# Splitting all 24 weight pieces of a mixture-of-experts step, with the second activation half converted one piece earlier

## The chip, the cores and the metric

The kernel runs on one core of a Trainium2 chip. The metric is the time on the device in microseconds (us) of one execution of the whole block; the shown time of a kernel is the median of its runs. The profile is one further execution, taken by the hardware profiler, which has a time of its own.

## The reference

One decoder layer with 1024 tokens and a width of 1024, all in float32. First a mixer (attention with a window of 128, and a linear recurrent branch, joined by gates), then a mixture of experts, then a last RMSNorm. The change touches the mixture of experts alone:

```python
logits = t @ w_router + b_router
top_val, top_idx = lax.top_k(logits, 4)          # 4 of 32 experts for each token
gate = softmax(top_val)
# for each expert e and its tokens xc, in chunks of 128 rows
gu = xc @ w_gate_up[e] + b_gate_up[e]            # 1024 -> 2048
g, u = gu[:, :1024], gu[:, 1024:]
g = minimum(g, 7); u = clip(u, -7, 7)
act = (u + 1) * (g * sigmoid(1.702 * g))
y = act @ w_down[e] + b_down[e]                  # 1024 -> 1024
out[token] += gate * y
```

## The kernel before, in words

**Steps.** After the mixer and the router the kernel runs a loop of steps (the loops `Fori(0, MAXS // 2)`, two steps u = 0, 1 in each turn, the guard `If(j < total)`). A step is one expert with up to 128 of its tokens. With these inputs there are 32 steps, one for each expert. An expert that has between 1 and 32 tokens more than a chunk holds has these computed in the same step as its tail (`If(tail > 0)`), by products of 32 rows each (`tail_product`, L676). Five engines run the same list of steps, each with its own program, and meet at semaphores.

**Weights.** An expert has six units of weights of 2 MB: units 0 and 2 are the gate columns, 1 and 3 the up columns, 4 and 5 the down projection. SyncE requests them by DMA (L362) into `ring`, each as soon as the step before has done with the same unit (`unit_mm[i]`). A unit is used in four pieces of 128x1024 numbers, which are numbered n = 0 to 23 in the order of their use (`sub_unit`): pieces 0 to 3 are unit 0, 4 to 7 unit 1, 8 to 11 unit 2, 12 to 15 unit 3, and 16 to 23 alternate in pairs between units 4 and 5.

**Split pieces.** A piece is multiplied by the rows of the tokens in one of two ways. A *split* piece is written as a high part and the remainder, both of type float32r: ScalarE copies the piece from `ring` to `w_hi` (function `high`, L900), VectorE subtracts that copy from the piece and writes `w_lo` (`low`, L1463), and TensorE runs six matmuls of 512 columns: twice rows_hi by w_hi, rows_lo by w_hi (L659, L660), and rows_hi by w_lo (L663). The buffers `w_hi` and `w_lo` have four places (NBUF = 4), so `high` of a piece waits (`sub_mm`) until TensorE has finished the split piece four before it. The rows themselves were split in the same way at the start of the step (`rows_hi` L892, `rows_lo` L1467), and so is the activation, in two halves: `actT_out` writes `act_hi` (ScalarE, L923), `actT_low` writes `act_lo` (VectorE, L1509).

**Native pieces.** Pieces 7 and 15 (`NATIVE`) are not split. TensorE multiplies them straight from `ring` as float32 (L650), by `rows_f`, a plain float32 copy of the last 256 contraction rows that ScalarE makes for each step (L891, in `rowsT_out`). Nothing is converted for these two; `SPLIT` lists the 22 others, and the index m of a piece in that list numbers the buffers and the semaphore counts.

**What else the engines do between pieces.** Everything is written out by hand, in program order on each engine; n is the piece after whose conversion, or before whose product, the work stands.

- TensorE, before piece n: n = 12 and n = 18: waits for half 0 or 1 of the activation (`act_done`) and transposes it (L687). n = 16 and n = 20: waits for `act_lo_done` of half 0 or 1. n = 16 also: two tail products. n = 20 also: transposes the rows of the next step (L621). After the last piece of a unit: a bias product (L642), which raises `unit_mm`.
- ScalarE, after `high` of piece n: n = 8: sigmoid of gate half 0 (L919). n = 16: `actT_out(0)`, then the sigmoid of gate half 1. n = 21: `actT_out(1)`. After piece 23: the rows of the next step, its pieces 0 to 3, and the two halves of the output (L927).
- VectorE, after `low` of piece n: n = 9: gate part 0 (L1483, L1485). n = 11: up part 0 (L1490, L1492). n = 16: `actT_low(0)`. n = 17: gate part 1. n = 18: up part 1, whose last instruction (L1492) raises `act_done` for the transposes before piece 18. n = 19: the tail's part. n = 21: `actT_low(1)`. After piece 23: `rows_lo` of the next step and its pieces 0 to 3.

```python
# TensorE, L683 on                              # ScalarE, L899
if n in ACT_T:        # (12, 18)                act.wait_ge(sub_mm, j * NSP + m + 1)
    pe.wait_ge(act_done, j * 2 + half + 1)      # VectorE, L1462
    ... 4 transposes, L687                      dve.wait_ge(hi_done, j * NSP + m + 1)
```

Of the kernel before, what the change touches and what calls it, by code (L numbers as in the profile page):

```python
# [6 lines left out]
P = 128  # L7
NT = SEQ // P
KD = D // P
HALF = 512  # L10
# [15 lines left out]
SUBS = 24  # L26
NATIVE = (7, 15)
SPLIT = tuple(n for n in range(SUBS) if n not in NATIVE)
NSP = len(SPLIT)
NBUF = 4  # L30
# [14 lines left out]
def hybrid_decoder_block(nc, x, positions, norm_mix_g, w_in, conv_w, conv_b, w_rg, b_rg, w_ig, b_ig,  # L45
# [25 lines left out]
    with ctx:  # L71
# [130 lines left out]
        rows_f = take(2 * P)  # L202
# [201 lines left out]
        def _(pe):  # L404
            mm = nc.tensor.matmul
# [229 lines left out]
            with pe.Fori(0, MAXS // 2) as pair:  # L635
                for u in range(2):
                    j = pair * 2 + u
                    with pe.If(j < total):
# [6 lines left out]
                        def piece(n):  # L645

                            i, k0 = sub_unit(n)
                            if n in NATIVE:
                                for q in range(2):
                                    last = mm(bank(i), rows_f[:, q * P:(q + 1) * P], wu[i][:, k0 + q, :], start=False, stop=False)  # L650
                            else:
                                m = SPLIT.index(n)
                                buf = (m + u * NSP) % NBUF
                                hi, lo = (rows_hi, rows_lo) if i < 4 else (act_hi, act_lo)
                                pe.wait_ge(hi_done, j * NSP + m + 1)
                                for q in range(2):
                                    ks = slice((k0 + q) * P, (k0 + q + 1) * P)
                                    wh = w_hi[:, buf, q * HALF:(q + 1) * HALF]
                                    mm(bank(i), hi[:, ks], wh, start=(k0 + q == 0), stop=False)  # L659
                                    mm(bank(i), lo[:, ks], wh, start=False, stop=False)  # L660
                                pe.wait_ge(lo_done, j * NSP + m + 1)
                                for q in range(2):
                                    last = mm(bank(i), hi[:, (k0 + q) * P:(k0 + q + 1) * P], w_lo[:, buf, q * HALF:(q + 1) * HALF],  # L663
                                              start=False, stop=False)
                                last.then_inc(sub_mm, 1)
                            if k0 + 2 == KD:
                                if i == 0:
                                    pe.wait_ge(sel_ready, j + 1)
                                bias(bank(i), i, 0, HALF, P).then_inc(unit_mm[i], 1)
# [56 lines left out]
        def _(act):  # L726
# [163 lines left out]
            def rowsT_out():  # L890
                act.activation(rows_f, bank(7)[:, 2 * P:4 * P], ACT.Copy)  # L891
                act.activation(rows_hi[:], bank(6, 2), ACT.Copy).then_inc(rowsT_done, 1)  # L892

            def high(m, u, j):

                i, k0 = sub_unit(SPLIT[m])
                if k0 == 0:
                    wait_reg(act, w_arrived[i], j * 16 + 16)
                act.wait_ge(sub_mm, j * NSP + m + 1)  # L899
                act.activation(w_hi[:, (m + u * NSP) % NBUF, :], place[i][:, k0 * HALF:(k0 + 2) * HALF], ACT.Copy).then_inc(hi_done, 1)  # L900

# [3 lines left out]
            for m in range(NBUF):  # L905
                high(m, 0, 0)
# [4 lines left out]
            with act.Fori(0, MAXS // 2) as pair:  # L911
                for u in range(2):
                    j = pair * 2 + u
                    with act.If(j < total):
# [14 lines left out]

                        for m in range(NBUF, NSP):  # L930
                            n = SPLIT[m]
                            high(m, u, j)
# [13 lines left out]
                            if n == 21:  # L946
                                actT_out(1)
# [3 lines left out]
                        with act.If(more > 0):  # L951
                            wait_reg(act, rowsT_mm, j + 2)
                            rowsT_out()
                            high(0, 1 - u, j + 1)
                        wait_reg(act, added, j * 16 + 16)
                        output(0)
                        with act.If(more > 0):
                            high(1, 1 - u, j + 1)
                            high(2, 1 - u, j + 1)
                        output(1)  # L960
                        with act.If(more > 0):
                            high(3, 1 - u, j + 1)
# [182 lines left out]
        def _(dve):  # L1145
# [312 lines left out]
            def low(m, u, j):  # L1458

                i, k0 = sub_unit(SPLIT[m])  # L1460
                buf = (m + u * NSP) % NBUF
                dve.wait_ge(hi_done, j * NSP + m + 1)  # L1462
                v.tensor_tensor(out=w_lo[:, buf, :], in0=place[i][:, k0 * HALF:(k0 + 2) * HALF],  # L1463
                                in1=w_hi[:, buf, :].bitcast(f32), op=ALU.subtract).then_inc(lo_done, 1)
# [8 lines left out]
            for m in range(NBUF):  # L1473
                low(m, 0, 0)
            with dve.Fori(0, MAXS // 2) as pair:
                for u in range(2):
                    j = pair * 2 + u
                    with dve.If(j < total):
# [34 lines left out]
                        for m in range(NBUF, NSP):  # L1513
                            n = SPLIT[m]
                            low(m, u, j)
# [15 lines left out]
                            if n == 21:  # L1531
                                actT_low(1)
                        with dve.If(more > 0):
                            dve.wait_ge(rowsT_done, j + 2)
                            rows_low()
                            for m in range(NBUF):
                                low(m, 1 - u, j + 1)
# [38 lines left out]
```

## Time and profile before

| | |
|---|---|
| median of 3 runs | 2251.74 us (2250.1 to 2253.74) |
| the profiled execution: its own time | 2247.22 us |
| the profiled execution: span of the core | 2245.6 us |
| mean granted clock of TensorE | 0.971 of 2.4 GHz |
| busy over the span: TensorE, VectorE, ScalarE, GpSimd | 94%, 66%, 53%, 13% |
| the 32 steps of experts | from 810 us to 2208 us of the span |

How to read it: the span runs from the first instruction of the program to the last. "PE" is TensorE's matmuls, "PEld" its loads of stationary operands, "DVE" VectorE, "ACT" ScalarE, "POOL" GpSimd, "SP" SyncE. An engine's busy time is what its records cover. Records of following instructions of one engine overlap a little, so the pace of an engine is read from start to start. L1463 is line 1463 of the kernel before.

### The profile page before, as it was taken

The page shows a single profiled execution, that of the slowest core. Times are in us where ns is not written, and L with a number is a line of the kernel's source. Part 1 is how long each engine was busy: PE and PEld are TensorE (multiplying, and loading weights), DVE is VectorE, ACT ScalarE, POOL GpSimd, SP SyncE. Part 2 cuts the span into 40 slices and gives each one's busy share as a digit, 9 for nine tenths or more (in the row PEclk, how much of TensorE's full clock was granted, in tenths as well). Part 3 has the DMA queues.
Part 4 walks back from the last instruction along what each step waited for, and adds up shares of the span by engine and source line. Part 5 has one row for each costly group of instructions (what it writes and reads, how often), then busy time and mean ns, then how long its engine had stood idle before and what let it go on. Part 6 is the DMA issues. An engine that isn't in the chain of part 4 may idle for free.

```text
span 2245.6 us, 35483 instructions
## 1 busy us (share of the span) xinstructions
PE 2109.2 (94%) x11224; PEld 1474.1 (66%) x11225; DVE 1491.8 (66%) x1900; ACT 1195.0 (53%) x1623; POOL 282.7 (13%) x334
## 2 busy tenths in 40 slices
PE   7989988999989669999999999999999999999993
PEld 4445555767668547777777677776777777776772
DVE  4326654555444557877877668977877887876784
ACT  3152434334333336666756557766665766765674
POOL 3010000000002410110222101111211010210000
PEclk9999999999999779999999999999999999999997
DMA  7110020110043576987977779978979979976994
GB/s 224 38 38 0 22 75 1 38 38 19 20 169 113 157 228 227 353 297 277 371 271 255 245 280 380 373 261 285 355 252 332 370 264 375 345 256 242 373 344 158
DMA packets 247678, 489.51 MB, mean 218 GB/s; under 512 B 19915, under 2 KB 29991, under 8 KB 247536
## 3 DMA queue, kind: packets, MB, share of 16 engines
q1 hardware_dynamic: 218768, 439.37, 54.2%
q0 software_dynamic: 21088, 49.35, 8.3%
q10 hardware_dynamic: 7776, 0.19, 0.2%
q8 instruction: 27, 0.44, 0.1%
q14 instruction: 19, 0.16, 0.0%
HBM read 461.01 MB, written 32.05 MB: 220 GB/s over the span
## 4 chain that ended last, share of the span: by engine, by line
PE 90%; DVE 4%; issue 3%; DMA 1%; SPq 1%; ACT 1%; POOL 0%; POOLq 0%; ACTq 0%; DVEq 0%
PE psum L659 15%; PE psum L660 14%; PE psum L663 14%; PE psum L676 8%; PE psum L427 5%; PE psum L552 5%; PE psum L650 5%; PE psum L540 3%; PE psum L542 3%; PE psum L535 3%; PE psum L642 2%; PE psum L451 2%; PE psum L495 2%; PE psum L621 2%; PE psum L597 1%
## 5 line engine op out<-in xcount | busy, mean ns | idle before, releaser
L1463 DVE TENSOR_TENSOR w_lo<-ring,w_hi 128x1024 fp32r<-128x1024 f32 x704 | 850.3, 1222 | 162.8 <-ACT w_hi L900 142.1
L900 ACT ACTIVATE w_hi<-ring 128x1024 fp32r<-128x1024 f32 x704 | 741.0, 1061 | 349.2 <-PE psum L663 337.4
L659 PE MATMUL psum<-w_hi,rows_hi 128*128 128x512 f32 x896 | 372.1, 415 | 4.2 <-DVE rows_lo L1467 2.7
L660 PE MATMUL psum<-w_hi,rows_lo 128*128 128x512 f32 x896 | 350.4, 391 | 0.0
L663 PE MATMUL psum<-w_lo,rows_hi 128*128 128x512 f32 x896 | 277.0, 390 | 0.0
L659 PE MATMUL psum<-w_hi,act_hi 128*128 128x512 f32 x512 | 220.0, 430 | 0.3 <-issue 0.3
L659 PEld LDWEIGHTS psum<-w_hi,rows_hi 128*128 128x128 f32 x896 | 169.5, 189 | 52.2 <-issue 20.9
L660 PE MATMUL psum<-w_hi,act_lo 128*128 128x512 f32 x512 | 202.4, 395 | 0.0
L663 PEld LDWEIGHTS psum<-w_lo,rows_hi 128*128 128x128 f32 x896 | 168.5, 188 | 36.2
L660 PEld LDWEIGHTS psum<-w_hi,rows_lo 128*128 128x128 f32 x896 | 169.2, 189 | 32.9
L676 PE MATMUL psum<-ring,region_m 128*32 128x256 f32 x3072 | 174.2, 380 | 0.0
L663 PE MATMUL psum<-w_lo,act_hi 128*128 128x512 f32 x512 | 160.9, 395 | 0.0
L1295 DVE TENSOR_TENSOR h_lo<-ring,h_hi 128x1024 fp32r<-128x1024 f32 x64 | 78.4, 1225 | 118.3 <-ACT g_hi L822 118.3
L1131 POOL DMA_INDIRECT acc_rows<-region_m,meta x32 | 53.6, 1676 | 804.3 <-ACT region_m L927 734.7
L676 PEld LDWEIGHTS psum<-ring,region_m 128*32 128x32 f32 x3072 | 95.9, 110 | 73.5 <-issue 13.8
L819 ACT ACTIVATE h_hi<-ring 128x1024 fp32r<-128x1024 f32 x64 | 68.1, 1064 | 136.6 <-PE psum L542 136.6
L650 PE MATMUL psum<-ring,region_a 128*128 128x512 f32 x256 | 120.2, 592 | 0.0
L659 PEld LDWEIGHTS psum<-w_hi,act_hi 128*128 128x128 f32 x512 | 96.9, 189 | 27.9 <-issue 10.4
L663 PEld LDWEIGHTS psum<-w_lo,act_hi 128*128 128x128 f32 x512 | 96.2, 188 | 23.3
L552 PE MATMUL psum<-ring 128*128 128x512 f32 x256 | 111.2, 592 | 0.0
L427 PE MATMUL psum<-ring 128*128 128x512 f32 x256 | 110.1, 592 | 0.8 <-DVE ring L1167 0.8
L660 PEld LDWEIGHTS psum<-w_hi,act_lo 128*128 128x128 f32 x512 | 96.7, 189 | 17.8
(289 smaller groups left out, 2747.8 us busy)
## 6 DMA issues: line engine op xcount, KB each, us to landing
ring<-in_w_gate_up_dram SPq DMA_DIRECT2D x128, 2048.0 KB, 14.9
ring<-in_w_down_dram SPq DMA_DIRECT2D x64, 2048.0 KB, 11.4
ring<-in_w_in_dram SPq DMA_DIRECT2D x9, 1024.0 KB, 8.1
ring<-in_w_in_dram SPq DMA_DIRECT2D x3, 2048.0 KB, 22.8
region_m<-in_x_dram SPq DMA_DIRECT2D x8, 512.0 KB, 9.8
ring<-in_w_out_dram SPq DMA_DIRECT2D x2, 2048.0 KB, 7.6
region_a<-in_x_dram POOLq DMA_DIRECT2D x8, 512.0 KB, 4.7
acc_rows<-region_a POOLq DMA_DIRECT2D x8, 512.0 KB, 2.9
```

Of the source, the lines that this page charges most:

```text
L427: last = mm(bank(4 + n % 4), w[:, k, m * P:(m + 1) * P], hT[:, k, th * HALF:(th + 1) * HALF], start=(k == 0), stop=(k == KD - 1))
L535: mm(bank(2 * th + q), g_hi[b][:, q * P:(q + 1) * P], h_hi[b][:, th * HALF:(th + 1) * HALF], start=first, stop=False)
L552: last = mm(bank(4 + 2 * th + q), w[:, k, j * P:(j + 1) * P], x_[:, k, th * HALF:(th + 1) * HALF], start=(k == 0), stop=(k == GROUP - 1))
L650: last = mm(bank(i), rows_f[:, q * P:(q + 1) * P], wu[i][:, k0 + q, :], start=False, stop=False)
L659: mm(bank(i), hi[:, ks], wh, start=(k0 + q == 0), stop=False)
L660: mm(bank(i), lo[:, ks], wh, start=False, stop=False)
L663: last = mm(bank(i), hi[:, (k0 + q) * P:(k0 + q + 1) * P], w_lo[:, buf, q * HALF:(q + 1) * HALF], start=False, stop=False)
L676: mm(dst[TAIL * q:TAIL * (q + 1), :], stat_of(k), wu[i][:, k, c:c + QC], start=(k == 0), stop=False)
L819: act.activation(h_hi[b][:], hT[:, k, :], ACT.Copy)
L900: act.activation(w_hi[:, (m + u * NSP) % NBUF, :], place[i][:, k0 * HALF:(k0 + 2) * HALF], ACT.Copy).then_inc(hi_done, 1)
L1295: v.tensor_tensor(out=h_lo[b][:], in0=hT[:, k, :], in1=h_hi[b][:].bitcast(f32), op=ALU.subtract)
L1463: v.tensor_tensor(out=w_lo[:, buf, :], in0=place[i][:, k0 * HALF:(k0 + 2) * HALF], in1=w_hi[:, buf, :].bitcast(f32), op=ALU.subtract).then ...
```

## The change

All 24 pieces of a step become split pieces. `NATIVE`, `SPLIT`, `NSP`, the copy `rows_f` and its conversion are gone; the buffer of a piece is n % 4, and the semaphore counts go by 24 in a step. `actT_out(1)` on ScalarE and `actT_low(1)` on VectorE stand after piece 20, where they stood after piece 21. The order of TensorE's work stays, except that pieces 7 and 15 are six float32r matmuls each.

```diff
--- before.py
+++ after.py
@@ -24,9 +24,6 @@
 UNIT = KD * HALF
 SHIFT = 4
 SUBS = 24
-NATIVE = (7, 15)
-SPLIT = tuple(n for n in range(SUBS) if n not in NATIVE)
-NSP = len(SPLIT)
 NBUF = 4
 TAIL_ROWS_AT, TAIL_GU_AT, TAIL_ACT_AT, NEXT_ROWS_AT = 13, 16, 21, 20
 ACT_T = (12, 18)
@@ -199,7 +196,6 @@
         gsig = [take(HALF) for _ in range(2)]
         act_rows = [take(HALF) for _ in range(2)]
         glu = take(HALF)
-        rows_f = take(2 * P)
         tail_sig, tail_act, tail_glu, yrow_t = (take(QC) for _ in range(4))
         assert at[0] <= A_COLS - 2 * D
 
@@ -645,24 +641,19 @@
                         def piece(n):
 
                             i, k0 = sub_unit(n)
-                            if n in NATIVE:
-                                for q in range(2):
-                                    last = mm(bank(i), rows_f[:, q * P:(q + 1) * P], wu[i][:, k0 + q, :], start=False, stop=False)
-                            else:
-                                m = SPLIT.index(n)
-                                buf = (m + u * NSP) % NBUF
-                                hi, lo = (rows_hi, rows_lo) if i < 4 else (act_hi, act_lo)
-                                pe.wait_ge(hi_done, j * NSP + m + 1)
-                                for q in range(2):
-                                    ks = slice((k0 + q) * P, (k0 + q + 1) * P)
-                                    wh = w_hi[:, buf, q * HALF:(q + 1) * HALF]
-                                    mm(bank(i), hi[:, ks], wh, start=(k0 + q == 0), stop=False)
-                                    mm(bank(i), lo[:, ks], wh, start=False, stop=False)
-                                pe.wait_ge(lo_done, j * NSP + m + 1)
-                                for q in range(2):
-                                    last = mm(bank(i), hi[:, (k0 + q) * P:(k0 + q + 1) * P], w_lo[:, buf, q * HALF:(q + 1) * HALF],
-                                              start=False, stop=False)
-                                last.then_inc(sub_mm, 1)
+                            buf = n % NBUF
+                            hi, lo = (rows_hi, rows_lo) if i < 4 else (act_hi, act_lo)
+                            pe.wait_ge(hi_done, j * SUBS + n + 1)
+                            for q in range(2):
+                                ks = slice((k0 + q) * P, (k0 + q + 1) * P)
+                                wh = w_hi[:, buf, q * HALF:(q + 1) * HALF]
+                                mm(bank(i), hi[:, ks], wh, start=(k0 + q == 0), stop=False)
+                                mm(bank(i), lo[:, ks], wh, start=False, stop=False)
+                            pe.wait_ge(lo_done, j * SUBS + n + 1)
+                            for q in range(2):
+                                last = mm(bank(i), hi[:, (k0 + q) * P:(k0 + q + 1) * P], w_lo[:, buf, q * HALF:(q + 1) * HALF],
+                                          start=False, stop=False)
+                            last.then_inc(sub_mm, 1)
                             if k0 + 2 == KD:
                                 if i == 0:
                                     pe.wait_ge(sel_ready, j + 1)
@@ -888,22 +879,21 @@
 
 
             def rowsT_out():
-                act.activation(rows_f, bank(7)[:, 2 * P:4 * P], ACT.Copy)
                 act.activation(rows_hi[:], bank(6, 2), ACT.Copy).then_inc(rowsT_done, 1)
 
-            def high(m, u, j):
-
-                i, k0 = sub_unit(SPLIT[m])
+            def high(n, j):
+
+                i, k0 = sub_unit(n)
                 if k0 == 0:
                     wait_reg(act, w_arrived[i], j * 16 + 16)
-                act.wait_ge(sub_mm, j * NSP + m + 1)
-                act.activation(w_hi[:, (m + u * NSP) % NBUF, :], place[i][:, k0 * HALF:(k0 + 2) * HALF], ACT.Copy).then_inc(hi_done, 1)
+                act.wait_ge(sub_mm, j * SUBS + n + 1)
+                act.activation(w_hi[:, n % NBUF, :], place[i][:, k0 * HALF:(k0 + 2) * HALF], ACT.Copy).then_inc(hi_done, 1)
 
             act.sem_inc(y_done)
             act.sem_inc(ty_done)
             act.activation(ssq[:, 2, 0:1], eps, ACT.Sigmoid)
-            for m in range(NBUF):
-                high(m, 0, 0)
+            for n in range(NBUF):
+                high(n, 0)
             act.wait_ge(rowsT_mm, 1)
             rowsT_out()
             act.wait_ge(table_done, 1)
@@ -927,9 +917,8 @@
                             act.activation(yrow[u][:, half * HALF:(half + 1) * HALF], bank(4 + half), ACT.Copy,
                                            scale=meta[:, u, 1:2].bitcast(f32)).then_inc(y_done, 1)
 
-                        for m in range(NBUF, NSP):
-                            n = SPLIT[m]
-                            high(m, u, j)
+                        for n in range(NBUF, SUBS):
+                            high(n, j)
                             if n == 8:
                                 sigmoid(0)
                             if n == 16:
@@ -943,7 +932,7 @@
                                 with act.If(tail > 0):
                                     wait_reg(act, tgate_mm, before + 2)
                                     act.activation(tail_sig, bank(1)[:, 0:QC], ACT.Sigmoid, scale=ALPHA).then_inc(tgsig_done, 1)
-                            if n == 21:
+                            if n == 20:
                                 actT_out(1)
                         with act.If(tail > 0):
                             wait_reg(act, tactT_mm, before + 1)
@@ -951,15 +940,15 @@
                         with act.If(more > 0):
                             wait_reg(act, rowsT_mm, j + 2)
                             rowsT_out()
-                            high(0, 1 - u, j + 1)
+                            high(0, j + 1)
                         wait_reg(act, added, j * 16 + 16)
                         output(0)
                         with act.If(more > 0):
-                            high(1, 1 - u, j + 1)
-                            high(2, 1 - u, j + 1)
+                            high(1, j + 1)
+                            high(2, j + 1)
                         output(1)
                         with act.If(more > 0):
-                            high(3, 1 - u, j + 1)
+                            high(3, j + 1)
                         with act.If(tail > 0):
                             wait_reg(act, tdown_mm, before + 2)
                             wait_reg(act, tadded, before * 16 + 16)
@@ -1455,13 +1444,12 @@
             def selector(u, e):
                 v.tensor_copy(sel_cur[0:96, u, :], eq[0:96, ds(e, 1)].to_broadcast([96, P])).then_inc(sel_ready, 1)
 
-            def low(m, u, j):
-
-                i, k0 = sub_unit(SPLIT[m])
-                buf = (m + u * NSP) % NBUF
-                dve.wait_ge(hi_done, j * NSP + m + 1)
-                v.tensor_tensor(out=w_lo[:, buf, :], in0=place[i][:, k0 * HALF:(k0 + 2) * HALF],
-                                in1=w_hi[:, buf, :].bitcast(f32), op=ALU.subtract).then_inc(lo_done, 1)
+            def low(n, j):
+
+                i, k0 = sub_unit(n)
+                dve.wait_ge(hi_done, j * SUBS + n + 1)
+                v.tensor_tensor(out=w_lo[:, n % NBUF, :], in0=place[i][:, k0 * HALF:(k0 + 2) * HALF],
+                                in1=w_hi[:, n % NBUF, :].bitcast(f32), op=ALU.subtract).then_inc(lo_done, 1)
 
             def rows_low():
                 v.tensor_tensor(out=rows_lo[:], in0=bank(6, 2), in1=rows_hi[:].bitcast(f32),
@@ -1470,8 +1458,8 @@
             selector(0, 0)
             dve.wait_ge(rowsT_done, 1)
             rows_low()
-            for m in range(NBUF):
-                low(m, 0, 0)
+            for n in range(NBUF):
+                low(n, 0)
             with dve.Fori(0, MAXS // 2) as pair:
                 for u in range(2):
                     j = pair * 2 + u
@@ -1510,9 +1498,8 @@
                                             in1=act_hi[:, half * HALF:(half + 1) * HALF].bitcast(f32),
                                             op=ALU.subtract).then_inc(act_lo_done, 1)
 
-                        for m in range(NBUF, NSP):
-                            n = SPLIT[m]
-                            low(m, u, j)
+                        for n in range(NBUF, SUBS):
+                            low(n, j)
                             if n == 4:
                                 selector(1 - u, e_next)
                             if n == 9:
@@ -1528,13 +1515,13 @@
                             if n == 19:
                                 with dve.If(tail > 0):
                                     tail_glu_part()
-                            if n == 21:
+                            if n == 20:
                                 actT_low(1)
                         with dve.If(more > 0):
                             dve.wait_ge(rowsT_done, j + 2)
                             rows_low()
-                            for m in range(NBUF):
-                                low(m, 1 - u, j + 1)
+                            for n in range(NBUF):
+                                low(n, j + 1)
                         dve.nop()
 
             for t in range(NT):
```

## Rows read from the trace of the kernel before

**Rows 1.** The page: busy time of TensorE, and the shares of the last chain.

```profile
PE 2109.2 (94%) x11224; PEld 1474.1 (66%) x11225; DVE 1491.8 (66%) x1900; ACT 1195.0 (53%) x1623; POOL 282.7 (13%) x334
...
PE 90%; DVE 4%; issue 3%; DMA 1%; SPq 1%; ACT 1%; POOL 0%; POOLq 0%; ACTq 0%; DVEq 0%
```

**Rows 2.** Windows: PE, PEld, DVE, ACT, POOL busy us (records), PE clock, DMA share, GB/s.

```profile
1435.85:1473.21 37.36, 37.07 (x164) 28.13 (x164) 33.37 (x35) 27.65 (x30) 6.84 (x9) 1.00 1.04 370
1473.21:1523.31 50.10, 49.68 (x378) 35.12 (x378) 37.68 (x41) 29.84 (x35) 8.80 (x10) 1.00 0.72 251
```

**Rows 3.** Groups by line: busy us, mean ns of one, then idle before them.

```profile
L1463 DVE TENSOR_TENSOR w_lo<-ring,w_hi 128x1024 fp32r<-128x1024 f32 x704 | 850.3, 1222 | 162.8 <-ACT w_hi L900 142.1
...
L676 PE MATMUL psum<-ring,region_m 128*32 128x256 f32 x3072 | 174.2, 380 | 0.0
...
L650 PE MATMUL psum<-ring,region_a 128*128 128x512 f32 x256 | 120.2, 592 | 0.0
```

**Rows 4.** Timeline of TensorE, step without tail: start us, us, operation, idle before.

```profile
1453.46 0.60 PE L687 MATMUL psum<-ident,region_a 128*128 128x128 f32 x4
...
1455.29 0.39 PE L659 MATMUL psum<-w_hi,rows_hi 128*128 128x512 f32 x1
...
1456.65 0.39 PE L659 MATMUL psum<-w_hi,rows_hi 128*128 128x512 f32 x1
...
1458.01 1.88 PE L650 MATMUL psum<-ring,region_a 128*128 128x512 f32 x4
1459.73 0.38 PE L642 MATMUL psum<-region_s,region_m 96*128 96x512 bf16 x1
...
1461.34 0.40 PE L659 MATMUL psum<-w_hi,act_hi 128*128 128x512 f32 x1
...
1462.74 0.60 PE L687 MATMUL psum<-ident,region_a 128*128 128x128 f32 x4
...
1466.43 1.06 PE L621 MATMUL psum<-ident,region_m 128*128 128x128 f32 x8 [0.29 <-issue]
```

**Rows 5.** Timeline of ScalarE in the same step.

```profile
1453.43 1.06 ACT L900 ACTIVATE w_hi<-ring 128x1024 fp32r<-128x1024 f32 x1 [0.30 <-PE psum L663]
1454.40 0.58 ACT L923 ACTIVATE act_hi<-psum 128x512 fp32r<-128x512 f32 x1
1454.87 0.59 ACT L919 ACTIVATE region_a<-psum 128x512 f32<-128x512 f32 x1
1455.49 1.06 ACT L900 ACTIVATE w_hi<-ring 128x1024 fp32r<-128x1024 f32 x1
```

**Rows 6.** Timeline of VectorE in the same step.

```profile
1449.60 0.69 DVE L1492 SCALAR_TENSOR_TENSOR region_a<-region_a 128x512 f32<-128x512 f32 x1
...
1456.59 1.22 DVE L1463 TENSOR_TENSOR w_lo<-ring,w_hi 128x1024 fp32r<-128x1024 f32 x1 [0.24 <-ACT w_hi L900]
1457.73 0.42 DVE L1483 TENSOR_SCALAR region_a<-region_a 128x512 f32<-128x512 f32 x1
1458.18 0.69 DVE L1485 SCALAR_TENSOR_TENSOR region_a<-psum,region_a 128x512 f32<-128x512 f32 x1
1458.79 1.22 DVE L1463 TENSOR_TENSOR w_lo<-ring,w_hi 128x1024 fp32r<-128x1024 f32 x1
1460.15 0.69 DVE L1490 TENSOR_SCALAR region_a<-psum 128x512 f32<-128x512 f32 x1
1460.87 0.69 DVE L1492 SCALAR_TENSOR_TENSOR region_a<-region_a 128x512 f32<-128x512 f32 x1
```

**Rows 7.** Timeline at the first step's start, granted clock at its lower level.

```profile
808.72 1.23 DVE L1467 TENSOR_TENSOR rows_lo<-psum,rows_hi 128x1024 fp32r<-128x1024 f32 x1 [22.36 <-ACT rows_hi L892]
...
810.08 0.79 PE L659 MATMUL psum<-w_hi,rows_hi 128*128 128x512 f32 x1 [2.73 <-DVE rows_lo L1467]
...
811.09 0.63 PE L659 MATMUL psum<-w_hi,rows_hi 128*128 128x512 f32 x1
...
811.52 0.63 PE L660 MATMUL psum<-w_hi,rows_lo 128*128 128x512 f32 x1
```

## The prediction

> **What bounds the kernel now.** I read the page first: TensorE is busy for 94% of the span, and the chain that ended last is 90% TensorE [rows 1]. Over a stretch such a share can hide much, so I then looked at single steps. There are two kinds. A native piece leaves four records on L650, so its 256 records are 64 pieces, two in each of 32 steps; a tail leaves 192 records on L676, so its 3072 are 16 tails [rows 3]. Sixteen steps have a tail and take about 50 us, sixteen have none and take 37.4 us [rows 2]. In both TensorE is covered but for 0.3 to 0.4 us. So in the expert loop the product stream sets the time, and a microsecond taken out of it counts, as long as nothing else is late.
>
> How near is the next engine? In the step without tail VectorE is busy 33.37 of 37.36 us, in the one with tail 37.68 of 50.10 [rows 2]. The reader should see that the two kinds differ: in one VectorE has 4 us to spare, in the other 12. For a sum over a whole step 4 us are plenty; for a chain of dependent work inside it they need not be, and the change touches such a chain.
>
> **Part 1: the products.** A split piece takes TensorE 1.36 us from start to start (1455.29 to 1456.65), a native one 1.72 us (1458.01 to 1459.73) [rows 4]. Each of the 64 exchanged pieces saves 0.36 us: 0.72 us in each step, 23.0 us in all, if TensorE never waits.
>
> The Trainium skill ("TensorE: Matmul & The Clock Gate", Back-to-back issue gap) gives about 216 ns for an isolated 512-column matmul at full clock, against the 227 ns that 1.36 / 6 makes here. By it a split piece would be 1.29 us and the saving 27 us; the row decides.
>
> **Part 2: the conversions.** Each step gains two `high` (1.06 us) on ScalarE and two `low` on VectorE. The record of a `low` is 1.22 us, but back to back its pace is 1.14 us (1456.59 to 1457.73) [rows 6]. VectorE's load without tail rises from 33.4 to 35.7 us against a TensorE step of 37.36 - 0.72 = 36.64 us. As a sum it still fits, and with a tail easily. ScalarE, 27.65 us busy [rows 2], has room for 2.1 us more. The removed copy `rows_f` hid behind products; I cost it at nothing.
>
> **Part 3: the chain to the transposes before piece 18.** These wait for `act_done`, raised by the last L1492. Today that ends at 1461.56 and the transposes start at 1462.74 [rows 6, 4]: slack 1.18 us. Two things lengthen the chain. `high(16)` waited for the fourth *split* piece back, which was piece 11, because 15 was skipped; now it is piece 12. And `high(17)` stands behind `high(16)`, `actT_out(0)` and the sigmoid. Today these three ran early, and `high(17)` could start 0.20 us after piece 12 ended (1455.49 against 1455.29) [rows 5, 4]. Let P be the end of piece 12. After the change:
>
> - ScalarE: `high(16)` at P + 0.20, `actT_out(0)` 0.97 later, the sigmoid 0.47 later, `high(17)` 0.49 later (a record of 0.59 less the 0.10 by which its neighbours overlap), so at P + 2.13; it ends at P + 3.19 [rows 5].
> - VectorE: `low(17)` at P + 3.23, then 1.14 to L1483, 0.45 to L1485, 0.61 to `low(18)`, 1.14 to L1490, 0.72 to L1492 and 0.69 for itself [rows 6]: P + 7.98.
> - TensorE asks for it at P + 7.45 today (1462.74 - 1455.29), and at P + 7.09 with piece 15 shorter [rows 4].
>
> Add 0.13 us from VectorE's end to TensorE's start (809.95 to 810.08) [rows 7], and TensorE waits 7.98 + 0.13 - 7.09 = 1.02 us. No row of before shows that wait, so I bound it. With no delay at the semaphore it is 0.89 us. With every record laid end to end without overlap (0.20 + 1.06 + 0.58 + 0.59 + 1.06 + 0.04 + 1.22 + 0.42 + 0.69 + 1.22 + 0.69 + 0.69 = 8.46) it is 1.50 us. I take 1.02, since starts in the rows show the overlap at each of these pairs. Queued behind this wait are pieces 18 to 23 and the whole next step, so it counts in full. It comes once in each step without tail. In a step with tail two tail products stand between pieces 15 and 16, 174.2 / 48 = 3.6 us each [rows 3]; in these 7.2 us the chain finishes, and the step keeps its 0.72 us.
>
> The transposes before piece 12 wait in the same way for the first half, whose L1492 ends at 1450.29 and which is wanted at 1453.46 [rows 6, 4]: 3.17 us of slack. The added `low(7)` moves it back by 1.14 us and TensorE comes 0.36 us earlier; some 1.6 us are left, and I cost it at nothing.
>
> **Part 4: the moved half.** Piece 20 waits for `act_lo_done` of half 1. With the wait above, the transposes start at P + 8.11, and TensorE stands before piece 20 about 3.2 us later, P + 11.3 (today L621, just behind that point and with 0.29 us of idle time ahead of it, starts 3.69 us after the transposes) [rows 4]. ScalarE's `actT_out(1)` waits for the transposes and ends near P + 9.3; VectorE goes `low(19)` P + 7.9, `low(20)` 9.0, `actT_low(1)` 10.2 to 10.9. It is in time by 0.4 us. Behind `low(21)`, at its old place, it would be at 12.0 and cost another 0.7 us. So the move saves a new wait rather than time of before: nothing in the sum. On ScalarE `high(21)` stands behind that wait, and is 1 us later than it could be; piece 21 comes only near P + 14, so nobody feels it. No DMA is moved; SyncE's requests follow `unit_mm` and come earlier or later with TensorE.
>
> **The sum.** 32 x 0.72 = 23.0 us gained, 16 x 1.02 = 16.3 us given back: 6.7 us less. The profiled execution would go from 2247.2 to 2240.5 us. It lies 4.5 us under the median of the runs shown, so the median goes from 2251.7 to 2245.0 us. Steps without tail become 0.3 us *longer* (37.7), steps with tail 0.7 us shorter (49.4). About 0.2%, or 4.5 us, is what a measurement can tell from no change, and the forecast is just beyond it.
>
> **The rivals.**
>
> *The whole saving arrives.* If the chain were 1 us shorter than I add it up, TensorE would not wait: -23.0 us, 2229. For it: VectorE's sum fits, and TensorE waits for neither engine inside a step today. Against it: the rows give every link. A ceiling may also step in: without tail DMA already moves 370 GB/s at a share of 1.04 [rows 2], so a step of 36.64 us needs 2% more than it delivers now. Anything from 2229 to 2241: 0.18.
>
> *The wait is longer and eats the gain.* With 1.3 to 1.7 us in each of 16 steps the sum is -2.2 to +4.2 us. The end-to-end bound is 1.50. 0.12.
>
> *A second wait, and the kernel is slower.* The margin before piece 20 is 0.4 us. If `actT_low(1)` came 1.14 us later than worked out, one `low`, TensorE would wait 0.7 us more in each step without tail: -6.7 + 16 x 0.74 = +5.1 us, 2257. It decides from 0.4 us of lateness on, and the kernel is slower by over 0.2% from 0.7 us of added waiting. For it: VectorE at 35.7 of 37 us has hardly a pause in which to catch up. Against it: in the rows it does catch up before piece 20. 0.08.
>
> *The clock falls.* Today the granted clock is 1.00 in these stretches and TensorE's gaps are 0.3 us [rows 2, 4]. If idle microseconds in every step sent it to its lower level, a matmul would take 0.43 us (811.09 to 811.52) [rows 7] instead of 0.23: six pieces at it, 36 x 0.20, are 7 us in a step without tail, 16 x 7 - 7 = +105 us in all, 2357. One wait of 1 us in 37 is little beside what TensorE does around it, so 0.02. The Trainium skill ("TensorE: Matmul & The Clock Gate", A second HAM failure mode) describes such an oscillation with frequent short idles between groups of matmuls; no row here shows one in the loop.
>
> **How the numbers follow.** My own case, one wait of 0.8 to 1.3 us before piece 18, has 0.60 and spans -10.2 to -2.2 us: 2241.5 to 2249.5. The range 2233 to 2254 takes in the longer wait and half of the larger gains; outside stay the full gain (0.10) and the two slow cases (0.10). Faster by over 0.2% needs a wait under 18.5 / 16 = 1.16 us: 0.44 of my 0.60, and the first rival's 0.18, make 0.62. Same: 0.16 + 0.12 = 0.28. Slower: 0.10.
>
> **What would show it.** In the profile after, L650 and L891 are gone, and L900 and L1463 count 768. The group L687 shows idle time before it, released by VectorE's L1492 of before, 16 times about 1 us and never in a step with tail. Steps without tail take 37.7 us, with tail 49.4. No idle time released by `act_lo`, none by DMA. I am wrong if L687 shows no wait (full gain), if L621 or piece 20 shows one (second rival on the slow side), or if the steps with tail gain less than 0.7 us.

## The result, and the profile after

The changed kernel takes 2230.7 us (median of 6 runs, 2229.8 to 2231.3) against 2251.7 us for the kernel before on the same chip. The ratio is 0.9905, with a 95% interval of 0.9892 to 0.9918: 21 us less, between 18 and 24. The forecast was 2245.0 us, range 2233 to 2254. The direction was right; the gain is three times the one worked out, and outside the range.

The profiled execution took 2230.5 us. From its page, the lines that answer to [rows 1] and to the first of [rows 3]:

```profile
PE 2088.0 (94%) x11352; PEld 1494.9 (67%) x11353; DVE 1550.9 (70%) x1964; ACT 1244.1 (56%) x1655; POOL 291.4 (13%) x334
...
PE 84%; DVE 5%; issue 4%; ACT 2%; DMA 2%; SPq 1%; POOL 0%; ACTq 0%; DVEq 0%; POOLq 0%
...
L1451 DVE TENSOR_TENSOR w_lo<-ring,w_hi 128x1024 fp32r<-128x1024 f32 x768 | 915.0, 1221 | 144.2 <-ACT w_hi L890 132.7
```

TensorE's busy time fell by 21.2 us, and its share of the last chain from 90% to 84%: something else now stands in that chain. Next, two steps of the same kinds as in [rows 2], with the same columns:

```profile
1428.43:1465.72 37.29, 36.56 (x168) 28.62 (x168) 34.96 (x37) 29.00 (x31) 8.18 (x9) 1.00 1.05 374
1465.72:1514.72 49.00, 48.80 (x383) 35.89 (x382) 39.60 (x43) 31.46 (x36) 9.26 (x10) 1.00 0.74 255
```

The step without tail went from 37.36 to 37.29 us (forecast 37.7), the one with tail from 50.10 to 49.00 us (forecast 49.4). Both are 0.4 us shorter than forecast. With 16 steps of each kind that makes 16 x 0.07 + 16 x 1.10 = 18.7 us. (These are single steps; the 16 steps with tail take 799.8 us in the trace of before and 781.6 us in this one, 1.14 us less each.)

**The wait that was forecast is there.** First the changed kernel's group of transposes (L678 answers to L687), then timelines of the three engines in the step without tail, as in [rows 4 to 6]:

```profile
its engine sat idle before it (us, times) until:
  DVE region_a L1480: 30.4, 32
```

The 32 times are 16 waits, each counted once for the matmuls (16 times 0.73 us, 11.7 us) and once for the loads of the stationary operands.

```profile
1447.52 0.39 PE L650 MATMUL psum<-w_hi,rows_hi 128*128 128x512 f32 x1
...
1453.24 0.39 PE L650 MATMUL psum<-w_hi,act_hi 128*128 128x512 f32 x1
...
1455.54 0.66 PE L678 MATMUL psum<-ident,region_a 128*128 128x128 f32 x4 [0.73 <-DVE region_a L1480]
1455.95 0.48 PE L650 MATMUL psum<-w_hi,act_hi 128*128 128x512 f32 x1
...
1458.93 1.06 PE L617 MATMUL psum<-ident,region_m 128*128 128x128 f32 x8
```

```profile
1447.72 1.06 ACT L890 ACTIVATE w_hi<-ring 128x1024 fp32r<-128x1024 f32 x1 [1.00 <-PE psum L654]
1448.69 0.58 ACT L913 ACTIVATE act_hi<-psum 128x512 fp32r<-128x512 f32 x1
1449.17 0.59 ACT L909 ACTIVATE region_a<-psum 128x512 f32<-128x512 f32 x1
1449.64 2.01 ACT L890 ACTIVATE w_hi<-ring 128x1024 fp32r<-128x1024 f32 x2
```

```profile
1450.73 1.23 DVE L1451 TENSOR_TENSOR w_lo<-ring,w_hi 128x1024 fp32r<-128x1024 f32 x1
...
1454.79 0.69 DVE L1480 SCALAR_TENSOR_TENSOR region_a<-region_a 128x512 f32<-128x512 f32 x1
...
1457.67 0.68 DVE L1497 TENSOR_TENSOR act_lo<-psum,act_hi 128x512 fp32r<-128x512 f32 x1
```

Piece 12 ends at P = 1447.52. `high(16)` starts at P + 0.20, `high(17)` at P + 2.12, `low(17)` at P + 3.21, and the last L1480 ends at 1455.48, P + 7.96; the forecast had 0.20, 2.13, 3.23 and 7.98. Piece 17 and the wait last 2.30 us (1453.24 to 1455.54) where piece 17 alone took 1.40 (1461.34 to 1462.74 in [rows 4]), and the transposes then take 0.41 us to the next piece instead of 0.35. That is a loss of 0.96 us in each step without tail, against 1.02 forecast. (The profile prints 0.73 us, because it counts from the end of the last matmul's record, and back-to-back matmul records overlap.) In steps with tail there is none.

**What was not forecast** lies before piece 20. The end of piece 19 in the kernel before, TensorE and then VectorE:

```profile
1465.51 0.63 PE L663 MATMUL psum<-w_lo,act_hi 128*128 128x512 f32 x2
1466.43 0.73 PE L621 MATMUL psum<-ident,region_m 128*128 128x128 f32 x5 [0.29 <-issue]
```

```profile
1465.17 0.68 DVE L1509 TENSOR_TENSOR act_lo<-psum,act_hi 128x512 fp32r<-128x512 f32 x1
```

Two matmuls of piece 19 start from 1465.51 at a pace of 0.23 us, so L621 could have started at 1465.98. It started at 1466.43, 0.45 us later. The profile, which counts from the end of the last record at 1466.14, labels 0.29 us of this "issue", a wait for nothing that it shows. But `act_lo` was finished only at 1465.85, 0.13 us before L621 could have started. The prediction passed over that gap. The first three experiments ask whether it was a wait.

### The profile page after: what moved, and what is told of

Read it like the earlier page. It is cut to its first block, busy times and chain, and to the rows that moved or that the text cites. A ratio compares the mean times of both kernels' runs of the same rounds, so it can differ in the third digit from the quotient of the medians.

```text
span 2228.9 us, 36027 instructions
## 1 busy us (share of the span) xinstructions
PE 2088.0 (94%) x11352; PEld 1494.9 (67%) x11353; DVE 1550.9 (70%) x1964; ACT 1244.1 (56%) x1655; POOL 291.4 (13%) x334
## 4 chain that ended last, share of the span: by engine, by line
PE 84%; DVE 5%; issue 4%; ACT 2%; DMA 2%; SPq 1%; POOL 0%; ACTq 0%; DVEq 0%; POOLq 0%
PE psum L650 14%; PE psum L651 14%; PE psum L654 14%; PE psum L667 8%; PE psum L423 5%; PE psum L548 5%; PE psum L536 3%; PE psum L538 3%; PE psum L531 3%; PE psum L638 2%; PE psum L447 2%; PE psum L491 2%; PE psum L593 1%; PE psum L617 1%; PE psum L594 1%
## 5 line engine op out<-in xcount | busy, mean ns | idle before, releaser
L1451 DVE TENSOR_TENSOR w_lo<-ring,w_hi 128x1024 fp32r<-128x1024 f32 x768 | 915.0, 1221 | 144.2 <-ACT w_hi L890 132.7
L890 ACT ACTIVATE w_hi<-ring 128x1024 fp32r<-128x1024 f32 x768 | 803.7, 1059 | 277.7 <-PE psum L654 269.0
L650 PE MATMUL psum<-w_hi,rows_hi 128*128 128x512 f32 x1024 | 422.6, 413 | 4.3 <-DVE rows_lo L1455 2.5
L651 PE MATMUL psum<-w_hi,rows_lo 128*128 128x512 f32 x1024 | 400.4, 391 | 0.0
L654 PE MATMUL psum<-w_lo,rows_hi 128*128 128x512 f32 x1024 | 316.6, 390 | 0.0
L650 PEld LDWEIGHTS psum<-w_hi,rows_hi 128*128 128x128 f32 x1024 | 194.1, 190 | 47.0 <-issue 10.5
L654 PEld LDWEIGHTS psum<-w_lo,rows_hi 128*128 128x128 f32 x1024 | 192.7, 188 | 41.3
L651 PEld LDWEIGHTS psum<-w_hi,rows_lo 128*128 128x128 f32 x1024 | 193.5, 189 | 37.7
L536 PE MATMUL psum<-h_hi,g_lo 128*128 128x512 f32 x256 | 100.7, 393 | 0.4 <-DVE g_lo L1287 0.4
```

Of the source, the lines that this page charges most:

```text
L536: mm(bank(2 * th + q), g_lo[b][:, q * P:(q + 1) * P], h_hi[b][:, th * HALF:(th + 1) * HALF], start=False, stop=False)
L890: act.activation(w_hi[:, n % NBUF, :], place[i][:, k0 * HALF:(k0 + 2) * HALF], ACT.Copy).then_inc(hi_done, 1)
L1451: v.tensor_tensor(out=w_lo[:, n % NBUF, :], in0=place[i][:, k0 * HALF:(k0 + 2) * HALF], in1=w_hi[:, n % NBUF, :].bitcast(f32), op=ALU.subt ...
```

## The experiments

A ratio below is the time of a run over that of the kernel before on the same chip, with its 95% interval.

### 1. All pieces split, the second half left where it was

```diff
 ScalarE, after high(n):   VectorE, after low(n):
-if n == 20:               -if n == 20:
-    actT_out(1)           -    actT_low(1)
+if n == 21:               +if n == 21:
+    actT_out(1)           +    actT_low(1)
```

(Changed kernel as the base.) Expected:

> All 24 pieces split, but the second activation half converted after piece 21 as before the change. Theory A (the move took away a hidden wait of 0.45 us before piece 20 in every step, and keeps a larger one away): back come 0.45 us in each of the 16 steps with tail and 1.13 us in each of the 16 without, 25 us in all: about 2256 us, slower than the kernel before. Steps with tail 49.4 us, without 38.4 us. Rival B (no such wait before; the exchanged native pieces gave more than their rows show): steps with tail stay at 48.9 us, those without lose the 0.7 us of the prediction, about 2242 us.

Measured: ratio 1.0022 (1.0012 to 1.0032), 2252.6 us against 2247.4 us for the kernel before on that chip. Splitting the two pieces *without* the move makes the kernel slower, by 5 us (3 to 7). Steps take 38.43 and 49.4 us, as theory A has it, and rival B's 48.9 us with tail is not met. TensorE and VectorE in a step without tail:

```profile
1466.53 0.63 PE L654 MATMUL psum<-w_lo,act_hi 128*128 128x512 f32 x2
1468.22 0.84 PE L617 MATMUL psum<-ident,region_m 128*128 128x128 f32 x6 [1.07 <-DVE act_lo L1497]
```

```profile
1466.96 0.69 DVE L1497 TENSOR_TENSOR act_lo<-psum,act_hi 128x512 fp32r<-128x512 f32 x1
```

Here the profile names the releaser. In a step with tail the old pattern is back, with the old label:

```profile
887.13 0.63 PE L654 MATMUL psum<-w_lo,act_hi 128*128 128x512 f32 x2
888.04 1.06 PE L617 MATMUL psum<-ident,region_m 128*128 128x128 f32 x8 [0.28 <-issue]
```

### 2. The move alone, on the kernel before

```diff
 NATIVE = (7, 15)          # as before
-if n == 21: actT_out(1)   (ScalarE)     -if n == 21: actT_low(1)   (VectorE)
+if n == 20: actT_out(1)                 +if n == 20: actT_low(1)
```

> The kernel before with the move alone: pieces 7 and 15 stay native, the second half is converted after piece 20. Theory A: 0.45 us less in each of 32 steps, -14.4 us, about 2237 us; steps with tail 49.6 us, without 36.9 us; L621 comes 1.4 us after piece 19 begins, not 1.85. Rival B: no change, 2251.7 us. The prediction on record also says no change for this part.

Measured: ratio 0.9933 (0.9916 to 0.9950), 2232.5 us against 2247.4 us, 14.9 us less (11 to 19). The move by itself is worth some two thirds of the whole change. A step without tail takes 36.87 us, and L621 follows piece 19 at once, with no gap:

```profile
1457.00 0.63 PE L663 MATMUL psum<-w_lo,act_hi 128*128 128x512 f32 x2
1457.46 0.93 PE L621 MATMUL psum<-ident,region_m 128*128 128x128 f32 x7
```

```profile
1427.34:1464.21 36.87, 36.87 (x164) 28.21 (x164) 33.29 (x35) 27.43 (x30) 6.67 (x9) 1.00 1.05 376
```

So the 0.45 us was a wait for `act_lo`. In the trace of before it stands in all 32 steps, 0.43 to 0.48 us but for the first, where it is 0.54 (the last step has no next rows; there the first matmul of piece 20 is late): 32 x 0.45 = 14.4 us. Rival B, which laid the surplus on the native pieces, is out twice.

### 3. Pieces 3 and 7 native in place of 7 and 15

```diff
 (kernel of experiment 2)
-NATIVE = (7, 15)
+NATIVE = (3, 7)
-    if n == 4:
+    if n == 5:
         selector(1 - u, e_next)
```

The selector had to move because piece 4 is now converted in the step before.

> As the move alone, but the two native pieces are 3 and 7 instead of 7 and 15: the same number of conversions and the same products, only high(16) now waits for piece 12 and not 11. Theory A (the wait before the transposes of piece 18 comes from that chain): 0.95 us of waiting in the 16 steps without tail, none with tail, about 2253 us, 15 to 17 us over the move alone. Rival C (that wait comes from VectorE's higher load of 24 conversions): no wait, as the move alone, about 2237 us.

Measured: ratio 1.0003 (0.9993 to 1.0013), 2248.5 us, 16.0 us over experiment 2 on the same chip, with the same conversions and the same products. Two steps without tail, 37.98 us here against 36.87 there, and the transposes:

```profile
1436.42:1474.40 37.98, 37.25 (x165) 28.09 (x164) 32.98 (x35) 27.38 (x30) 8.19 (x9) 1.00 1.02 360
...
1464.22 0.66 PE L687 MATMUL psum<-ident,region_a 128*128 128x128 f32 x4 [0.73 <-DVE region_a L1492]
```

VectorE is busy no longer than in experiment 2 (32.98 against 33.29 us), and the wait is the full one of the changed kernel. Before `low(16)` VectorE even stands idle, until ScalarE has done `high(16)`:

```profile
1457.51 1.23 DVE L1463 TENSOR_TENSOR w_lo<-ring,w_hi 128x1024 fp32r<-128x1024 f32 x1 [0.84 <-ACT w_hi L900]
```

Here, then, the wait does not come from VectorE's load (rival C), but from the piece for which `high(16)` waits. In the changed kernel the two can't be told apart so well. There VectorE runs `low(12)` to `low(16)` without a pause:

```profile
1444.22 5.83 DVE L1451 TENSOR_TENSOR w_lo<-ring,w_hi 128x1024 fp32r<-128x1024 f32 x5
```

At its pace of 1.14 us it would reach `low(16)` at 1444.22 + 4 x 1.14 = 1448.78, and `high(16)` ends at 1448.78 too (1447.72 + 1.06). VectorE's backlog is thus as late as ScalarE's wait for piece 12, and an earlier `high(16)` alone would have given back little. With the 0.18 us of experiment 7 it would be some 0.2 of the 0.96 us, an estimate from these rows; no run tried it. This case also prices the exchange of native pieces: it differs from the changed kernel by two native pieces ahead of the chain, with the same waits, and its step is 37.98 - 37.29 = 0.69 us longer.

### 4. Up part 1 one piece earlier

```diff
 if n == 17:
     gate_part(1)
-if n == 18:
     up_part(1)
```

(Changed kernel as the base, also in what follows.)

> The changed kernel with up part 1 directly behind gate part 1, after piece 17, nothing else moved. Theory A: act_done comes 1.14 us earlier and the wait before the transposes of piece 18 goes, but VectorE's low(18) to low(20) still stand ahead of actT_low(1), which now is late by itself: L617 starts 1.1 us later than TensorE could, the wait moves to piece 20, steps without tail stay at 37.3 us, and the time within 0.2% of the changed kernel's. Rival E (the wait is only that of the transposes): it goes, steps without tail 36.3 us, 15 us less.

Measured: 0.9914 of the kernel before (0.9900 to 0.9927), beside 0.9908 (0.9894 to 0.9922) for the changed kernel on the same chip: the same within the intervals. The transposes show no idle time any more, and in steps without tail the wait stands before piece 20:

```profile
1456.25 0.63 PE L654 MATMUL psum<-w_lo,act_hi 128*128 128x512 f32 x2
1457.77 1.06 PE L617 MATMUL psum<-ident,region_m 128*128 128x128 f32 x8 [0.89 <-DVE act_lo L1497]
```

```profile
1456.51 0.68 DVE L1497 TENSOR_TENSOR act_lo<-psum,act_hi 128x512 fp32r<-128x512 f32 x1
```

TensorE was 0.96 us earlier at piece 20 and VectorE was not. A wait removed from a chain gives nothing while the next thing on that chain is equally late.

### 5. Up part 1 and actT_low(1) earlier

```diff
 if n == 17:
     gate_part(1)
-if n == 18:
     up_part(1)
 if n == 19:
     with dve.If(tail > 0):
         tail_glu_part()
-if n == 20:
     actT_low(1)
```

> As the last one, and actT_low(1) after piece 19 too: two moves on VectorE, none on ScalarE. Theory A: both waits go, steps without tail 36.2 us, 16 to 17 us less than the changed kernel, the same as with the sigmoid moved too.

Measured: ratio 0.9837 (0.9824 to 0.9850), 2213.5 us against 2251.0 us for the kernel before and 2228.8 us for the changed one on that chip. No matmul of the transposes waits any more, nor does one of L617 inside the loop, and steps without tail take 36.2 us. This beats both kernels.

### 6. The same, with gate part 1 and the sigmoid earlier too

```diff
 ScalarE                           VectorE
+if n == 15: sigmoid(1)             if n == 16: actT_low(0); + gate_part(1)
 if n == 16: actT_out(0)           -if n == 17: gate_part(1)
-            sigmoid(1)            +if n == 17: up_part(1)
                                   +if n == 19: tail part; actT_low(1)
```

> The changed kernel with work of the chain taken forward: ScalarE's sigmoid of half 1 after piece 15, VectorE's gate part 1 behind actT_low(0) after piece 16, up part 1 after piece 17, actT_low(1) after piece 19. Theory A: up part 1 ends some 0.4 us before TensorE asks for it, the wait of 0.95 us and the 0.1 us before piece 20 go in the 16 steps without tail, -16.9 us, about 2214 us, steps without tail 36.3 us. Rival D (without tail the DMA rate or VectorE's load sets 37.3 us, and the wait only shows where that surfaces): no change, 2231 us, with waits at other places (DMA, or w_lo).

Measured: ratio 0.9844 (0.9827 to 0.9860), 2212.4 us on the chip where the kernel before took 2247.4 us: as experiment 5 within the intervals. A step without tail:

```profile
1418.61:1454.82 36.21, 36.21 (x168) 28.78 (x168) 34.76 (x37) 29.02 (x31) 7.99 (x9) 1.00 1.05 376
```

TensorE is covered for all of it, VectorE for 96%. DMA moves 376 GB/s at a share of 1.05 in such steps and still nothing waits for weights: rival D, and the ceiling that the prediction held possible at 36.64 us, do not bind at 36.21 us.

### 7. The sigmoid alone earlier

```diff
 ScalarE
+if n == 15: sigmoid(1)
 if n == 16:
     actT_out(0)
-    sigmoid(1)
```

> The changed kernel with the sigmoid of half 1 after piece 15 instead of 16, on ScalarE alone. high(17) starts 0.47 us earlier, but VectorE reaches low(17) only behind actT_low(0), 0.15 to 0.2 us before it does now. Theory A, with VectorE next in line: the wait before the transposes shrinks from 0.95 to some 0.8 us and no more. Rival F (ScalarE's order alone sets it): it shrinks to 0.5 us.

Measured in the trace of one execution: the gap before the transposes goes from 0.73 to 0.55 us, so the wait from 0.96 to 0.78. (One more line stands in this program, so L1481, L1498 and L1452 answer to L1480, L1497 and L1451.)

```profile
1452.31 0.66 PE L678 MATMUL psum<-ident,region_a 128*128 128x128 f32 x4 [0.55 <-DVE region_a L1481]
```

```profile
1446.92 0.68 DVE L1498 TENSOR_TENSOR act_lo<-psum,act_hi 128x512 fp32r<-128x512 f32 x1
1447.52 1.22 DVE L1452 TENSOR_TENSOR w_lo<-ring,w_hi 128x1024 fp32r<-128x1024 f32 x1
```

`low(17)` starts at the pace of VectorE's own work behind `actT_low(0)`. ScalarE was the later of the two by 0.18 us only. Shortening ScalarE's path by 0.47 us uncovered VectorE's. The remaining 0.78 us is on both paths, ScalarE's from piece 12 and VectorE's backlog (see experiment 3).

### 8. The size of the difference, once more

> The changed kernel once more, to time it on the chip of the next ones. Its trace showed 16.7 us less than the kernel before and its median 21.0 us less; the kernel before was 2251.7 us there and 2247.4 us in the runs since. If the trace has the mechanisms complete (steps with tail 1.14 us shorter, without tail 0.06 us), the difference here lies near 17 to 19 us; if something outside the traced steps gives the rest, it stays at 21 us.

Measured: ratio 0.9908 (0.9894 to 0.9922), 22.2 us between medians. Then two more profiles of the kernel before and one of the changed kernel, on one chip:

> The kernel before, profiled again. Its profiled execution took 2247.2 us while the median of its runs was 2251.7 us, so medians give the change 21 us and the two traces 16.7 us. If the loop of steps has always the same length (1398.4 us), the missing 4 us lie ahead of or behind the loop and belong to the run, not to the change. If the loop is longer here (1401 us and more), it has waits that the first trace did not catch.

> As the one before it: a third profile of the kernel before, for the spread of the stretches from one execution to the next.

> The changed kernel, profiled on the same chip as the two before it. The loop of steps should again be 1379.7 to 1380.1 us long, and the difference to the kernel before in the loop 18 to 19 us.

From the first product of the first step to the last of the last step, the kernel before takes 1398.4, 1399.4 and 1399.8 us in its three profiles, the changed kernel 1380.1, 1379.7 and 1379.1 us. So the loop gives 18 to 21 us, 19.6 between the means (1399.2 and 1379.6). Most of that spread lies in the first step, which takes 39.2 to 40.0 us in either kernel. The loop starts anywhere between 810.1 and 813.0 us in these six profiles, after the arrival of the first rows by DMA. The first profile of the kernel before happened to start early and to have the shortest loop, which is why it shows 16.7 us. The medians differ by 21.0 and 22.2 us. Outside the loop the six profiles show no difference between the kernels (37.0 to 37.6 us behind it in both), so where a further 1 or 2 us would come from, these runs can't tell.

## Why the prediction was wrong

- **The products** (part 1): right. 0.72 us in each step were forecast; experiment 3 shows 0.69 us.
- **The conversions** (part 2): right for a whole step. VectorE's load in the step without tail went from 33.4 to 35.0 us (35.7 forecast) and didn't bind as a sum; experiment 6 runs with 34.8 of 36.2 us. Inside the step it is another matter, see the next point.
- **The chain to the transposes before piece 18** (part 3): right in place, kind of step and nearly in size: 0.96 us against 1.02 us. The semaphore took 0.06 us (1455.48 to 1455.54), not the 0.13 us taken from the slower clock. The cause named, that `high(16)` waits for piece 12, is one that makes the wait by itself (experiment 3), and experiments 4 and 5 remove the wait. But the chain left out that VectorE comes to `low(16)` from a backlog, and in the changed kernel that is as late as `high(16)`. That the two coincide within some hundredths of a microsecond is luck; with a longer backlog the forecast of this wait would have been too small.
- **The moved half** (part 4) is the step that failed. It said that the move "saves a new wait rather than time of before: nothing in the sum". Experiment 2 shows 14.9 us for it alone. The row was there, in [rows 4], and the text used it: L621 with 0.29 us of idle time, labelled "issue", 3.69 us after the transposes. It is also all of the 0.3 us for which the first paragraph found TensorE not covered, and it makes the sentence "TensorE waits for neither engine inside a step today" wrong. I worked out when TensorE would *ask* in the changed kernel and didn't put the same question to the kernel before, where `act_lo` ended 0.57 us before L621 started. The slack of today was worked out for the two transposes and not for this wait.
- The other half of part 4, that the move keeps a new wait away, was right in direction: in experiment 1 L617 comes 1.13 us later than in the changed kernel in a step without tail, where 0.7 us had been forecast.
- **The margin of 0.4 us before piece 20** was worse than it looked. In the changed kernel L617 still starts 0.1 us late in steps without tail, since `act_lo` has to be ready some 0.6 us before L617 and not at it (see the last section).

Put together for a step without tail: -0.69 (products), -0.45 (move), +0.96 (transposes), +0.10 (rest of the wait before piece 20) = -0.08 us; the trace has -0.07. With tail: -0.69 - 0.45 = -1.14; the trace has -1.14 in the mean. Over the loop these terms give 16 x 0.08 + 16 x 1.14 = 19.5 us, beside the 19.6 us measured. The forecast with the one missing term added, 6.7 + 14.4 = 21.1 us, would have come near: its errors in the products and in the transposes are 1 us each and cancel, and the 16 x 0.10 us are not in it.

The rival "the whole saving arrives" named 2229 us, near the measured value, but by another mechanism: it said there would be no wait before the transposes, and there is one. The time alone would have spoken for it; the lengths of the two kinds of steps tell the mechanisms apart.

The rival of the falling clock is out. The granted clock was 1.00 in both stretches of the changed kernel and in a step without tail of experiment 1 (1436.58 to 1475.01), where TensorE idles twice in a step without tail, by 0.73 and 1.07 us. The oscillation that the Trainium skill describes for frequent short idles between groups of matmuls ("TensorE: Matmul & The Clock Gate", A second HAM failure mode) is not to be seen at this density of idles.

## What to carry to other kernels

Before a moved wait is costed at nothing, work out its slack in the kernel as it is: when the data is ready, when the engine asks, and what the row behind it shows. Treat a gap labelled "issue" as a candidate for a short wait as soon as a semaphore wait stands there in the program and the producer ends just before; the same gap in every step is worth its length times the number of steps. Where several engines are within some tenths of a microsecond of each other, expect a removed wait to turn up at the next meeting point, and move both.

## What the runs showed of the hardware that was not expected

A matmul that waits for VectorE directly starts 0.06 us after VectorE's end (L1480 ends at 1455.48, L678 starts at 1455.54). Before piece 20 the program has a conditional part between the wait and the matmul, and there the matmul starts 0.57 to 0.58 us after VectorE's end where it waits: 1465.85 to 1466.43 in the kernel before, 1458.35 to 1458.93 in the changed one, 1467.65 to 1468.22 in experiment 1, 1457.19 to 1457.77 in experiment 4. Over all steps but the first it is 0.56 to 0.62 us. With the data earlier, the conditional part costs TensorE nothing: in experiment 5 `act_lo` ends at 1450.06 and L617 starts 0.67 us later, at the normal pace behind piece 19. So the time from the semaphore through the conditional part is hidden as long as the wait is satisfied early enough, and adds some 0.5 us to a wait that is not. This explains why `act_lo`, ready 0.13 us before L621 could have started, still cost 0.45 us; that the profile put the gap down to "issue" for the same reason is likely, but not shown. In the last step of the kernel before the conditional part is skipped, and the first matmul of piece 20 comes 0.60 us after `act_lo` (2201.53 to 2202.13). So neither the transposes nor the second wait inside that part make the delay; which of the register, compare and branch instructions before it does, no run separates.
